# Splitting the recurrent stage's weights ahead, during the third feed-forward, through DRAM

## What is computed

```python
def swiglu(h, w_gu, w_down):
    u = h @ w_gu
    return (jax.nn.silu(u[..., :D_FF]) * u[..., D_FF:]) @ w_down
...
    gx, rx = ux[..., :D_RNN], ux[..., D_RNN:]
...
    rx = centred_dwconv(rx, conv_w, conv_b)
...
        ax, bx = rglru_coeffs(rx, gate_w[d], gate_b[d], lam[d])
...
        h_x = linear_scan(ax, bx, h_c[:, -1])
...
    yx = (jax.nn.gelu(gx) * (hs_x[0] + hs_x[1])) @ w_out
```

## Time and profile before

| | us |
|---|---|
| median of 3 runs (2822.62 to 2825.4) | 2823.81 |
| the profiled execution: its own time | 2823.51 |
| its span in the profile | 2821.7 |
| PE busy | 2680.0 (95% of the span) |
| DVE busy | 1472.0 (52%) |
| POOL busy | 886.7 (31%) |
| ACT busy | 771.8 (27%) |

### The profile page before, as it was taken

How to read it: one execution, slowest core, us unless ns; L and a number is a source line. 1 busy time by engine, 2 the same in 40 slices (tenths; PEclk the granted TensorE clock), 3 DMA queues, 4 the chain that set the end, 5 groups by cost and what they waited for, 6 DMA issues and landing times.

```text
span 2821.7 us, 40060 instructions
## 1 busy us (share of the span) xinstructions
PE 2680.0 (95%) x15151; PEld 2494.0 (88%) x15151; DVE 1472.0 (52%) x2479; ACT 771.8 (27%) x1044; POOL 886.7 (31%) x367
## 2 busy tenths in 40 slices
PE   6999999999989899999999999999998887899998
PEld 4999999999958899999998999999987775778887
DVE  6666466665373766556656234322258886532233
ACT  4111122222173322111123221111235664332222
POOL 1322232222332232322231333222324443344442
PEclk8999999999999999999999999999999998999999
DMA  6443334423301244334431223222211112233332
GB/s 211 132 126 116 95 121 128 125 73 79 105 24 30 75 136 125 110 101 128 127 113 56 65 61 114 70 62 66 73 37 56 52 52 60 68 97 98 89 105 81
DMA packets 413089, 256.87 MB, mean 91 GB/s; under 512 B 6653, under 2 KB 405846, under 8 KB 413014
## 3 DMA queue, kind: packets, MB, share of 16 engines
q1 hardware_dynamic: 413014, 255.87, 30.3%
HBM read 252.70 MB, written 4.25 MB: 91 GB/s over the span
## 4 chain that ended last, share of the span: by engine, by line
PE 63%; issue 19%; DVE 8%; POOL 5%; ACT 4%; DMA 0%; SPq 0%; POOLq 0%; DVEq 0%; ACTq 0%
PE pair_b L1702 29%; PE pair_a L1702 28%; POOL w_lo L710 5%; DVE ada_sums L1133 1%; DVE decay L1662 1%; DVE decay L1660 1%; PE pair_c L1784 1%; DVE h_lo L1284 1%; DVE gate_i L1656 1%; DVE root L1654 1%; ACT root L1073 1%; ACT decay L1071 1%; PE pair_c L2038 1%; PE pair_r L2056 1%; PE pair_a L1692 1%
## 5 line engine op out<-in xcount | busy, mean ns | idle before, releaser
L710 POOL TENSOR_TENSOR w_lo<-raw,w_hi 128x1024 fp32r<-128x1024 f32 (+3 forms) x302 | 818.5, 2711 | 1733.0 <-ACT w_hi L820 1733.0
L820 ACT ACTIVATE w_hi<-raw 128x1024 fp32r<-128x1024 f32 (+3 forms) x302 | 337.2, 1117 | 1216.5 <-PE pair_b L1702 661.2
L1173 DVE TENSOR_TENSOR work_g<-work_s,pair_b 128x768 f32<-128x768 f32 (+1 forms) x88 | 78.1, 888 | 660.0 <-PE pair_b L1702 499.4
L1133 DVE SCALAR_TENSOR_TENSOR ada_sums<-ada_raw,cvec,ada_sums 128x256 f32<-128x256 f32 x896 | 394.8, 514 | 0.0
L1702 PE MATMUL pair_a<-h_hi,w_hi 128*128 128x384 f32 x1312 | 342.1, 342 | 18.1 <-POOL w_lo L710 17.9
L1702 PE MATMUL pair_a<-h_lo,w_hi 128*128 128x384 f32 x1312 | 335.9, 337 | 0.0
L1702 PE MATMUL pair_a<-h_hi,w_lo 128*128 128x384 f32 x1312 | 335.0, 336 | 0.0
L1702 PE MATMUL pair_b<-h_hi,w_hi 128*128 128x384 f32 x1168 | 296.8, 335 | 0.0
L1702 PE MATMUL pair_b<-h_hi,w_lo 128*128 128x384 f32 x1168 | 296.6, 334 | 0.0
L1702 PE MATMUL pair_b<-h_lo,w_hi 128*128 128x384 f32 x1168 | 296.4, 334 | 0.0
L1702 PEld LDWEIGHTS pair_a<-h_hi,w_hi 128*128 128x128 f32 x1312 | 235.8, 190 | 30.4 <-issue 17.3
(11 more groups left out here) (290 smaller groups left out, 4261.4 us busy)
## 6 DMA issues: line engine op xcount, KB each, us to landing
raw<-in_ffn_w_gu_dram SPq DMA_DIRECT2D x176, 512.0 KB, 3.8
ada_raw<-in_ada_w_dram SPq DMA_DIRECT2D x64, 1024.0 KB, 5.1
raw<-in_ffn_w_down_dram SPq DMA_DIRECT2D x64, 704.0 KB, 4.6
raw<-in_rg_w_in_dram SPq DMA_DIRECT2D x20, 512.0 KB, 3.8
ada_first<-in_ada_w_dram SPq DMA_DIRECT2D x4, 2048.0 KB, 13.5
raw<-in_ab_w_in_dram SPq DMA_DIRECT2D x16, 512.0 KB, 4.0
raw<-in_rg_w_out_dram SPq DMA_DIRECT2D x8, 640.0 KB, 4.5
raw<-in_ab_w_out_dram SPq DMA_DIRECT2D x8, 512.0 KB, 4.2
```

The costliest lines, as they stand in the source:

```text
L710: nc.gpsimd.tensor_tensor(wl[:, par, 0:kt * P], raw[:, par, 0:kt * P], wh[:, par, 0:kt * P].bitcast(F32), ALU.subtract).then_inc(split_rea ...
L820: nc.scalar.activation(wh[:, par, 0:kt * P], raw[:, par, 0:kt * P], ACT.Copy).then_inc(hi_done, 1)
L1133: step = nc.vector.scalar_tensor_tensor(out=sums[v], in0=tiles(k), scalar=c_k, in1=sums[v], op0=ALU.mult, op1=ALU.add)
L1173: nc.vector.tensor_tensor(gbuf[:, 0, 0:W], sbuf[:, 0, 0:W], up, ALU.mult)\
```

## The change

The 50 half panels of the recurrent stage's u and g weights and gate matrices (units of 128x512) are split in the third feed-forward. SP loads a unit to `unit_raw` (two buffers), POOL multiplies it by one into `unit_hi` (fp32r) and subtracts into `unit_lo` (which shares the buffer of `unit_raw`), and SP stores both to DRAM. On POOL a unit stands ahead of each panel's low part, from the second pair of gu20 to the first pair of dn21: units 0 to 19 (u) in gu20, 20 to 27 (gates 0 to 7) in dn20, 28 to 47 (g) in gu21, 48 and 49 in dn21. In the recurrent stage SP loads high and low parts straight into `w_hi` and `w_lo`: u always in buffer 0, g and three of the gate matrices in buffer 1, the fourth matrix in `gate_weights_3`. These panels have neither `high` nor `low`. The 8 panels of rg_out still have both; their place in ACT's and POOL's order moves.

```diff
@@ SP @@
+            def load_unit(r, src):
+                sp.dma_start(unit_raw[r][:, :].rearrange("p (k n) -> p k n", n=P), src).then_inc(unit_landed[r], 16)
+            def store_unit(k, r, to):
+                sp.wait_ge(unit_done, k + 1)
+                sp.dma_start(to(0), unit_hi[:, :].bitcast(F32)).then_inc(unit_stored, 16)
+                sp.dma_start(to(1), unit_lo[r][:, :].bitcast(F32)).then_inc(unit_stored, 16)
...
-                    def gate_up(i, between):
-                        load(i * 2 + p0, 0, KD, gu[:, :, span(i * P + h * KC * P, P)])
-                        load(i * 2 + (p0 + 1), 1, KD, gu[:, :, span(i * P + (DFF + h * KC * P), P)])
+                    def gate_up(i, between, units=None):
+                        load(i * 2 + split_no(p0), 0, KD, gu[:, :, span(i * P + h * KC * P, P)])
+                        store = with_unit(units, i - 1, 0) if units else None
+                        load(i * 2 + (split_no(p0) + 1), 1, KD, gu[:, :, span(i * P + (DFF + h * KC * P), P)])
+                        if units:
+                            store()
+                            with_unit(units, i - 1, 1)()
                         between()
...
                     def down(i, between):
...
                         for r in range(2):
-                            load(i * 2 + (p0 + r), r, KC, dn[:, h * KC:(h + 1) * KC, span(i * (2 * P) + r * P, P)])
+                            load(i * 2 + (split_no(p0) + r), r, KC, dn[:, h * KC:(h + 1) * KC, span(i * (2 * P) + r * P, P)])
+                            if units:
+                                for store in stores:
+                                    store()
+                                stores = [with_unit(units, i, r)]
+                        for store in stores:
+                            store()
                         between()
...
-            load_u(P_RG, 0, 0)
-            load_g(P_RG + 1, 1, 0)
-            with sp.Fori(0, KR // 2 - 1) as i:
...
+            def load_u(n):
+                sp.wait_ge(panel_used, P_RG - 1 if n == 0 else u_panel(n - 1) + 1)
+                for s, tile in ((0, wh), (1, wl)):
+                    sp.dma_start(tile[:, 0, 0:KD * P].bitcast(F32), u_split[n, s]).then_inc(u_landed, 16)
+            def load_g(n):
+                sp.wait_ge(panel_used, P_RG if n == 0 else g_panel(n - 1) + 1)
...
+            def load_gates(n):
+                if n >= 1:
+                    sp.wait_ge(panel_used, gate_panel(n - 1) + 1)
...
+            sp.wait_ge(unit_stored, 50 * 32 + 1)
+            load_u(0)
+            load_g(0)
+            for n in range(1, KR):
+                load_u(n)
+                load_gates(n - 1)
+                load_g(n)
+            load_gates(KR - 1)
...
@@ POOL @@
+            def unit(k, r):
+                pool.wait_ge(unit_landed[r], (k - r) * 8 + 16)
+                pool.wait_ge(unit_stored, k * 32 + 1)
+                nc.gpsimd.tensor_tensor(unit_hi[:, :], unit_raw[r][:, :], all_ones, ALU.mult).then_inc(unit_hi_done, 1)
+                pool.wait_ge(unit_hi_done, k + 1)
+                nc.gpsimd.tensor_tensor(unit_lo[r][:, :], unit_raw[r][:, :], unit_hi[:, :].bitcast(F32), ALU.subtract)\
+                    .then_inc(unit_done, 1)
+            def unit_pairs(p0, start, count, kt, k0):
+                with pool.Fori(start, count) as i:
+                    for r in range(2):
+                        unit(i * 2 + (k0 - 2 * start + r), r)
                         low(i * 2 + (p0 + r), r, kt)
...
+            conv_low(0)
             for n in range(1, KR):
-                p = P_RG + 3 * n - 1
-                low(p, (n + 1) % 2, KD)
-                low(p + 1, n % 2, 4)
-                if n == 1:
-                    conv_low(0)
-                low(p + 2, (n + 1) % 2, KD)
                 if n >= 2:
                     y_low(n - 2)
                 conv_low(n)
-            low(P_RG + 3 * KR - 1, 1, 4)
+            low(split_no(P_RGOUT), 0, KR)
             y_low(KR - 2)
-            low(P_RGOUT, 0, KR)
-            low(P_RGOUT + 1, 1, KR)
+            low(split_no(P_RGOUT) + 1, 1, KR)
             y_low(KR - 1)
...
@@ ACT @@
-            high(P_RG + 2)
             u_rows(0)
-            high(P_RG + 3)
             gelu_rows(0)
             for n in range(1, KR):
-                high(P_RG + 3 * n + 1)
                 u_rows(n)
                 gelu_tanh(n - 1)
-                high(P_RG + 3 * n + 2)
                 gates(n - 1)
-                high(P_RG + 3 * n + 3)
+                if n == KR - 1:
+                    high(P_RGOUT)
                 gelu_rows(n)
-            high(P_RG + 3 * KR + 1)
             gelu_tanh(KR - 1)
             gates(KR - 1)
+            high(P_RGOUT + 1)
```

More of the change, by code:

```diff
@@ L94 @@
 QUAD = 32
-QUAD = 32
+MOST = 15
+UNIT = 512
 def trunk(nc, x, c, ctx_in, c_ctx, ada_w, ada_b, norm_g, w_gu, w_down, ab_in, ab_out, pool_w,
@@ L638, in _ @@
             ffn(2)
[L641 to L655, removed]
@@ L669, in _ @@
-            load_gates(p + 3, 1, KR - 1)
+            def load_u(n):
[4 more added lines that the diff above has]
+                sp.wait_ge(panel_used, P_RG if n == 0 else g_panel(n - 1) + 1)
+                for s, tile in ((0, wh), (1, wl)):
+                    sp.dma_start(tile[:, 1, 0:KD * P].bitcast(F32), g_split[n, s]).then_inc(g_landed, 16)
@@ new lines, in load_gates @@
+            def load_gates(n):
+                if n >= 1:
+                    sp.wait_ge(panel_used, gate_panel(n - 1) + 1)
+                for s, tile in ((0, wh), (1, wl)):
+                    sp.dma_start(tile[:, 1, KD * P:KC * P].bitcast(F32), gate_split[n, s, :, 0:3 * P]).then_inc(gates_landed, 16)
+                    sp.dma_start(gate_w3[:, s, :].bitcast(F32), gate_split[n, s, :, 3 * P:4 * P]).then_inc(gates_landed, 16)
+            sp.wait_ge(unit_stored, 50 * 32 + 1)
+            load_u(0)
@@ L672, in _ @@
                 for r in range(2):
-                    load(i * 2 + (P_RGOUT + r), r, KR, wro[:, :, span(i * (2 * P) + r * P, P)])
+                    load(i * 2 + (split_no(P_RGOUT) + r), r, KR, wro[:, :, span(i * (2 * P) + r * P, P)])
             ffn(3)
@@ L715, in pairs, with split_ahead @@
                     for r in range(2):
-                        low(i * 2 + (p0 + r), r, kt)
+                        low(i * 2 + (split_no(p0) + r), r, kt)
+            all_ones = bass.AP(tensor=ones[:, :].tensor, offset=ones[:, 0:1].offset, ap=[list(ones[:, 0:1].ap[0]), [0, UNIT]])
+            def unit(k, r):
[9 more added lines that the diff above has]
+                        unit(i * 2 + (k0 - 2 * start + r), r)
+                        low(i * 2 + (p0 + r), r, kt)
+            def split_ahead():
+                nc.gpsimd.memset(unit_hi[:, 0:1].bitcast(F32), 0.0).then_inc(unit_stored, 1)
+                low(first["gu20"], 0, KD)
+                low(first["gu20"] + 1, 1, KD)
+                unit_pairs(first["gu20"], 1, KC, KD, 0)
+                unit_pairs(first["dn20"], 0, KD // 2, KC, 20)
+                pairs(first["gu21"], 0, 1, KD)
+                unit_pairs(first["gu21"], 1, KC, KD, 28)
+                unit_pairs(first["dn21"], 0, 1, KC, 48)
+                pairs(first["dn21"], 1, KD // 2, KC)
             def ffn(f):
-                low(first[f"gu{f}0"], 0, KD)
-                low(first[f"gu{f}0"] + 1, 1, KD)
+                low(split_no(first[f"gu{f}0"]), 0, KD)
+                low(split_no(first[f"gu{f}0"]) + 1, 1, KD)
                 pairs(first[f"gu{f}0"], 1, KC, KD)
@@ L769, in _ @@
             ffn(1)
-            ffn(2)
-            low(P_RG, 0, KD)
-            low(P_RG + 1, 1, KD)
+            split_ahead()
             def conv_low(n):
@@ L1689, in passes, with passes_of @@
             def passes(dst, par, kk, hi, lo, start, stop):
-                w1, w2 = wh[:, par, kk * P:(kk + 1) * P], wl[:, par, kk * P:(kk + 1) * P]
+                return passes_of(dst, wh[:, par, kk * P:(kk + 1) * P], wl[:, par, kk * P:(kk + 1) * P], hi, lo, start, stop)
+            def passes_of(dst, w1, w2, hi, lo, start, stop):
                 nc.tensor.matmul(dst, w1, hi, start=start, stop=False)
```

154 lines of the change are left out of this document (109 added, 45 removed).

## The result

| | before | after |
|---|---|---|
| median, us | 2823.88 (4 runs, 2822.62 to 2825.4) | 2806.22 (4 runs, 2804.33 to 2806.72) |
| profiled execution, its own time / span | 2823.51 / 2821.7 | 2806.72 / 2804.9 |
| PE busy | 2680.0 | 2674.8 |
| DVE busy | 1472.0 | 1447.6 |
| POOL busy | 886.7 | 928.8 |

A forecast was written before the change was run, and what follows sets the result against it. TensorE was taken to hold 63% of the chain, with a cycle of DVE and ACT bounding the recurrent loop; -24.7 - 1.2 + 5.9 + 1.9 + 10 + 4.5 = -3.6 us gave 2820 us, range 2807 to 2833.

The forecast's parts named there:

- Items 1 and 2: Recurrent loop: blocks of 20.88 us by DVE and ACT, 22.6 by turns through PE's clock; together -24.7 us.
- the ring: Recurrent loop: the cycle of DVE and ACT work from root to root, 24.88 us a block, to become 20.88.
- Rival (b): Recurrent loop: PE's clock holds, -31.6 us, time 2813; chance 0.10.
- Items 3, 5 and 7: Loop loads: nothing; two rg_out splits in scans at the stage's end: +5.9 us; units in gu20, gu21, dn21: nothing.
- Items 4 and 6: Opening of the recurrent stage: -1.2 us; unit 0 in the norm before the third feed-forward: +1.9 us.
- Item 8: dn20: units and splits on POOL stop DVE's ada sums; +10 us for sum 0, +4.5 for sums 1 to 3.
- Rival (c): dn20: sums 1 to 3 miss the 0.2 us margin to the next split, +5.4 us each; chance 0.25.
- Rival (a): dn20: sum 0 loses only unit 22, +7.5 us instead of 14.5, time 2813; chance 0.18.

The follow-up runs named there:

- the filling: The changed kernel with 11 matmuls of unused result per block put into PE's wait for gelu in the recurrent loop: 2801.11 us.
- the kernel with two edits: The changed kernel with 11 unused matmuls in PE's wait for gelu and the first two rg_out panels' splits out of DVE's scans: 2796.36 us.

## Why the prediction was wrong

**Items 1 and 2, the loop, were right**: 20.88 us by the ring, longer by turns through PE's clock, -23.4 for -24.7. The slow intervals were 22.4 to 23.5 us instead of 22.6, since a g panel after a wait of 4 to 5.5 us took 7.1 to 8.2 us where I had 7.3. The single prices add up otherwise than written: put back, POOL's operations cost the loop 21.2 us, and ACT's split, which I had at 0.95 a block, nothing as long as the clock falls (shown by its return with and without the filling). Rival (b), the clock holds, did not come true; the filling shows that it would have given 167.1 for the eight intervals, the forecast's bound of -31.6.

**Items 3, 5 and 7 held.** PE never waited for a landing inside the loop. Two splits in the scans cost 2.6 us each (forecast 2.9), 4.5 in all for 5.9. **Items 4 and 6** (-1.7 for -1.2, +1.1 for +1.9) came out in sign and size, but item 4 can't be told from the clock: the same code took 46.8 us from PE's use of the sums of squares of the norm's second token half to root 0 in one profile and 44.2 in another, at a mean granted clock of 0.85 and 1.00.

**Item 8, dn20, failed: +2.9 for +14.5.** Of the 10 us for sum 0 PE's wait shows 0.8 (1.48 after 0.66). The forecast had named this sign of being wrong, ada waits under 3 us. Two assumptions in it broke, and they hang together.

- "Unit 22 stops it (2.4), so that it is not done when POOL splits the panel at 1735.14 (3.0 more)". The unit's data had not landed. SP issued that load at 1725.86, behind the ada load and a weight panel, and the operation began at 1733.21. The forecast gave the ada data a delay and let the unit run at once, though both stand in one queue. The run with the ada load first shows the other order: the unit was 2.5 us earlier, it and the split stopped the sum (10.34 us), and PE waited 5.4 us. The mechanism was possible; the timing was wrong.
- "A DVE operation stands still while POOL works", taken as POOL always having its way. It holds when POOL has begun. When DVE's operations follow each other without a gap and POOL arrives among them, either may happen. The trace of the kernel before shows it, in two places that I did not look at. Outside dn20, POOL's split of 1024 columns (2.38 us alone) met a running sum; POOL first, then DVE:

```profile
353.30 4.69 POOL L710 TENSOR_TENSOR w_lo<-raw,w_hi 128x1024 fp32r<-128x1024 f32 x1 [7.99 <-ACT w_hi L820]
...
984.02 6.08 POOL L710 TENSOR_TENSOR w_lo<-raw,w_hi 128x1024 fp32r<-128x1024 f32 x1 [10.73 <-ACT w_hi L820]
```

```profile
982.22 5.62 DVE L1133 SCALAR_TENSOR_TENSOR ada_sums<-ada_raw,cvec,ada_sums 128x256 f32<-128x256 f32 x14
```

There POOL waited and the sum lost nothing. The 8.60 us of the earlier trace rows came about otherwise: the split at 1747.88 began in the sum's first 0.6 us, while its two TENSOR_SCALAR operations ran, and the first of the 14 that follow waited, 3.46 us for 0.48. That is how it went in all 32 sums of dn20, over the 17 profiles, in which a split came at that point. I took meetings of this one kind, in which POOL was first, for the rule.

Sums 1 to 3 were to lose 1.5 us of PE each, 4.5 in all. They lost 1.26, 0.74 and 0 (the last one meets no unit, since the first pair of gu21 has none), 2.0. Sum 2 met a split and a unit, as forecast, and there only the size was off: the unit cost the sum 1.8 us, not 2.4 (two of its operations took 1.26 and 1.51 us for 0.48). The same meeting cost PE 0.73 to 0.78 us in every other profile that has it. Rival (c), the missed margin of 0.2 us, never came about: the next split came after the end of the sum each time (at 1761.05 for one that ended at 1760.8). Rival (a) said that sum 0 loses only unit 22, for 7.5 us in dn20; it lost not even that.

The Trainium skill (GPSIMD Engine Reference, Specifications) says that GpSimd shares its SBUF interfaces with VectorE and contends with VectorE instructions that have two SBUF inputs or run in a 2-port mode; the rows agree. They show it on both sides: a POOL operation that has begun keeps DVE's waiting (3.45 us for 0.48), and DVE operations that follow each other without a gap can keep one of POOL's waiting to the end of the chain (3.67 us for 1.04).

## What to carry to other kernels

Before pricing a collision of GpSimd and VectorE, look up every place in the trace where the two already meet, and sort them by who came first, and by how long VectorE had been running without a gap; a meeting in which the waiting side was the other one shows as a long operation on that other engine. Price a transfer by its place in its queue, behind every wait that the queue's own engine makes, and not by its own needs. Where a loop makes TensorE wait some microseconds, work out the block at both levels of its clock: an edit that only lengthens the wait may bring nothing, and a few matmuls without use can bring the whole gain.

## What the runs showed of the hardware that I had not expected

**Who stops whom goes by the time of arrival, with a narrow border.** Take the chain of 14 DVE operations of one ada sum, and count from the moment at which it began to run, or ran again after a stop. In the dn20 of all profiles with units, 14 POOL operations came within 1.91 us of that moment and not right behind another, and all 14 got in at once (1.04 to 1.31 us for an operation of 1.04). Of the 23 that came after 1.94 us or more, 22 waited the chain out; the other is the split at 1735.80 shown above. The same kernel shows both outcomes at the same place (unit 24 in sum 1: 1.15 us at 1.80, 4.55 us at 1.97). Outside dn20 it is alike: the split at 984.02, 1.80 us after its chain's start, waited in 14 of the 17 profiles and got in in 3, those at four other places, which came after 1.98 us or more, waited in all 68 cases, and one that came after 0.53 us got in in all 17. In the kernel before it is this one, POOL first, then DVE:

```profile
84.40 2.59 POOL L710 TENSOR_TENSOR w_lo<-raw,w_hi 128x1024 fp32r<-128x1024 f32 x1 [9.98 <-ACT w_hi L820]
```

```profile
83.87 7.77 DVE L1133 SCALAR_TENSOR_TENSOR ada_sums<-ada_raw,cvec,ada_sums 128x256 f32<-128x256 f32 x14
```

How long POOL has been idle is not what decides: in dn20 it grows with the time of arrival (over 4.9 us it waited in 14 of 14 cases, under 2.4 it got in in 12 of 12), but the split at 84.40 had been idle for 10 us. No experiment moved the arrival through the chain step by step. What makes the border is open, and so is why both outcomes occur at 1.80 us. When POOL issues one operation right behind another, the two engines take turns, one operation each.

**The clock falls elsewhere as well.** Kernels whose loop ran at full clock gave 1 to 4 us of it back behind it: from the third rg_out panel to the end the kernels with matmuls filled in took 439.8 to 442.8 us, that with only the rg_out splits moved 440.2, and all others 438.5 to 438.7. In the 80 us after that panel the kernel with two edits had a mean granted clock of 0.92, the changed kernel 0.94. PE's last wait in the norm there is 2.6 us in both the changed kernel and the one with 16 filling matmuls, and only in the latter is it followed by slow matmuls. Why was not tried.
